# A routed expert layer: experts ranked by their tokens on the chip, with 128, 64 or 32 slots for each

## The reference

```python
h = h + mixed @ w_out
ht = rms_norm(h, g_ffn)                        # 256 tokens x 1024
scores = sigmoid(ht @ w_router)                # 64 experts
biased = scores + router_bias
# the 4 best of 8 groups of experts (sum of the two best of each), then the 8 best experts in them
w = w / sum(w) * 2.5                           # the scores of the 8 chosen
gate = sum(one_hot(idx, 64) * w, axis=1)
a, b = ht @ e_w1[e], ht @ e_w3[e]              # 1024 x 256 each, for each expert e
routed = sum over e of (silu(a) * b * gate[:, e]) @ e_w2[e]     # 256 x 1024
out = h + routed + (silu(ht @ s_w1) * (ht @ s_w3)) @ s_w2       # one shared expert
```

## Time and profile before

| what | value |
|---|---|
| runs | 708.69 us median of 3 (705.74 to 709.54) |
| profiled execution, its own time | 705.52 us |
| its span | 703.8 us |
| mean granted TensorE clock | 0.979 |
| loads of expert weights from batch 0 on | from 118.9 us |
| first expert product | 195.7 us |
| HBM read | 232.85 MB |

### The profile page before, as it was taken

How to read it: one execution, slowest core, us unless ns; L and a number is a source line. 1 busy time by engine, 2 the same in 40 slices (tenths; PEclk the granted TensorE clock), 3 DMA queues, 4 the chain that set the end, 5 groups by cost and what they waited for, 6 DMA issues and landing times.

```text
span 703.8 us, 11436 instructions
## 1 busy us (share of the span) xinstructions
PE 660.4 (94%) x4381; PEld 301.8 (43%) x4381; DVE 328.5 (47%) x762; ACT 203.9 (29%) x376; POOL 22.2 (3%) x40
## 2 busy tenths in 40 slices
PE   3999989999899999999999889998898999989995
PEld 2455466646444434434434333443333434334342
DVE  3999851246814354353443433435334353443435
ACT  5132553202314224133232240422314133141321
POOL 2100031000200000000000000000000000000000
PEclk9999999997999999999999999999999999999999
DMA  9934451961259999999999999999999999999952
GB/s 226 345 117 195 61 190 62 424 248 60 90 209 381 423 408 391 422 420 424 419 423 423 420 423 422 421 422 420 424 422 421 423 420 423 423 420 423 420 209 61
DMA packets 48692, 235.37 MB, mean 334 GB/s; under 512 B 16112, under 2 KB 16144, under 8 KB 21904
## 3 DMA queue, kind: packets, MB, share of 16 engines
q1 hardware_dynamic: 48224, 235.07, 83.8%
q10 hardware_dynamic: 288, 0.02, 0.0%
q0 software_dynamic: 160, 0.00, 0.0%
HBM read 232.85 MB, written 1.05 MB: 332 GB/s over the span
## 4 chain that ended last, share of the span: by engine, by line
PE 56%; DMA 33%; DVE 4%; ACT 2%; issue 2%; SPq 2%; POOL 0%; ACTq 0%; DVEq 0%
PE bank L452 54%; DMA ring<-in_e_w 32%; SPq L319 1%; DMA ring<-in_d_skip 1%; SPq L320 1%; PE bank L776 1%; DVE wreg L1424 1%; DVE reg_d L1107 0%; DVE wreg L1107 0%; ACT reg_c L876 0%; DVE acc L1107 0%; PE bank L514 0%; ACT reg_a L876 0%; POOL reg_d L417 0%; DVE wreg L1110 0%
## 5 line engine op out<-in xcount | busy, mean ns | idle before, releaser
L452 PE MATMUL bank<-ring,wreg 128*64 128x512 f32 (+1 forms) x2128 | 366.0, 600 | 15.9 <-DMA ring<-in_e_w 15.3
L452 PEld LDWEIGHTS bank<-ring,wreg 128*64 128x64 f32 (+1 forms) x2128 | 110.2, 124 | 235.1 <-issue 206.4
L452 PE MATMUL bank<-wreg,reg_a 128*128 128x512 f32 (+1 forms) x224 | 95.2, 587 | 2.9 <-ACT reg_a L876 1.5
L1107 DVE TENSOR_TENSOR wreg<-wreg,bank 128x256 f32<-128x256 f32 x34 | 14.3, 422 | 165.2 <-ACT wreg L1038 165.2
L1113 DVE SCALAR_TENSOR_TENSOR reg_d<-bank,wreg,reg_b 128x512 f32<-128x512 f32 x68 | 47.9, 746 | 60.5 <-ACT reg_b L876 58.5
L1038 ACT ACTIVATE wreg<-bank 128x256 f32<-128x256 f32 x34 | 13.1, 384 | 197.6 <-PE bank L452 197.6
L452 PEld LDWEIGHTS bank<-wreg,reg_a 128*128 128x128 f32 x224 | 43.2, 212 | 47.3 <-issue 45.5
L876 ACT ACTIVATE reg_b<-bank,wreg 128x512 bf16<-128x512 f32 x68 | 43.0, 683 | 62.7 <-PE bank L452 62.7
L1107 DVE TENSOR_TENSOR reg_d<-reg_d,reg_b 128x1024 bf16<-128x1024 f32 x34 | 41.6, 1225 | 38.2 <-ACT reg_b L876 38.2
L452 PE MATMUL bank<-wreg,reg_c 128*128 128x128 bf16 x864 | 55.0, 219 | 1.1 <-DVE wreg L1497 0.8
L452 PEld LDWEIGHTS bank<-wreg,reg_c 128*128 128x128 bf16 x864 | 50.0, 98 | 5.0 <-ACT wreg L876 3.2
(11 more groups left out here) (181 smaller groups left out, 417.6 us busy)
## 6 DMA issues: line engine op xcount, KB each, us to landing
ring<-in_e_w SPq DMA_DIRECT2D x200, 1024.0 KB, 15.7
wreg<-in_w_in SPq DMA_DIRECT2D x4, 2048.0 KB, 14.3
wreg<-in_w_out SPq DMA_DIRECT2D x1, 4096.0 KB, 13.0
wreg<-in_s_w SPq DMA_DIRECT2D x3, 1024.0 KB, 7.2
wreg<-in_e_w SPq DMA_DIRECT2D x3, 1024.0 KB, 4.9
acc<-in_x SPq DMA_DIRECT2D x4, 256.0 KB, 4.8
wreg<-in_w_glu SPq DMA_DIRECT2D x1, 1024.0 KB, 5.3
reg_a<-in_e_w SPq DMA_DIRECT2D x1, 1024.0 KB, 10.4
```

Source lines behind the costliest of these rows:

```text
L452: return nc.tensor.matmul(out_, lhsT, rhs, start=start, stop=stop, **kw)
L1107: return nc.vector.tensor_tensor(out_, a, b, op)
```

## The change

Experts 0 to 7 keep their fixed places (batches 0 and 1). The other 56 are ranked on the chip by their tokens in both halves together. The first 4 are wide: two items of one expert (64 slots for each half, 128 columns) on one load of its weights. The next 28 are plain, one item each, as before. The last 24 are small: one item with 32 slots for both halves together (32 columns). What doesn't fit gets extra items as before. The order is: batches 0 and 1 plain (experts 0 to 7), 2 small, 3 wide (two experts), 4 small, 5 wide (two experts), then the plain ones and the extra items in a loop, and the remaining four batches of small ones.

A small batch has one product `up` with four column tiles of 32, one turn, and one `down` for both halves. The sort (`sort_experts`, `take_list` on VectorE, `count_extras`, `list_items` on TensorE) stands behind the first product of batch 0. The first gather waits for pgT_evac instead of route_ready. SP reads every expert number from batch 2 on into a register (`listed`), and loads batches 2 to 6 by `load_slots`. The shared expert's down product goes into the combine of the first of the last small batches. The tail batch of two items is gone.

```diff
+N_FIXED = 8
+N_WIDE = 4
+N_SMALL = 24
+N_PLAIN = E - N_FIXED - N_WIDE - N_SMALL
+MAX_EXTRA = 88
+N_AHEAD = 2
+FIRST_PLAIN = (N_FIXED + PLAIN_AT) // EB + N_AHEAD
+N_NORMAL = FIRST_PLAIN + N_PLAIN // EB
+N_LAST = N_SMALL // EB - N_AHEAD
+FIRST_BATCHES = ("plain", "plain", "small", "wide", "small", "wide")
...
@@ SP @@
-            load13(ringV[:, 0, 0:4096], 2 * EB, w13_in[0])
+            sp.wait_ge(S["route_ready"], 1)
+            smalls = listed(SMALL_AT)
+            load13(ringV[:, 0, 0:4096], smalls[0], w13_in[0])
             for s in early2:
-                load2(ringV[:, s, 4096:6144], 2 * EB + s, w2_in[s])
-            load_batch(list(range(2 * EB, 3 * EB)), 1, early13, early2)
-            with sp.Fori(3, NB) as b:
-                load_batch([b * EB + s for s in range(EB)], b - 1)
...
+                load2(ringV[:, s, 4096:6144], smalls[s], w2_in[s])
+            load_batch(smalls, 1, early13, early2)
+            def load_slots(before, *loads):
+                sp.wait_ge(S["up_done"], before * NPAIR + NPAIR)
+                for experts_of, pair in loads:
+                    for s in pair:
+                        load13(ringV[:, s, 0:4096], experts_of[s], w13_in[s])
+                sp.wait_ge(S["down_done"], before * 2 + 2)
+                for experts_of, pair in loads:
+                    for s in pair:
+                        load2(ringV[:, s, 4096:6144], experts_of[s], w2_in[s])
+            wides = listed(0, 2)
+            smalls = listed(SMALL_AT + EB)
+            plains = listed(PLAIN_AT)
+            load_slots(2, (wides, (0, 1)), (smalls, (2, 3)))
+            load_slots(3, (smalls, (0, 1)))
+            load_slots(4, (wides, (2, 3)), (plains, (0, 1)))
+            load_slots(5, (plains, (2, 3)))
+            x_before = sp.value_load(n_before[0:1, :], min_val=N_NORMAL - 2, max_val=N_NORMAL - 2 + MAX_FULL)
+            with sp.Fori(FIRST_PLAIN, x_before + 1) as before:
+                load_batch(listed(before * EB + (EB + PLAIN_AT - FIRST_PLAIN * EB)), before)
+            load_batch(listed(SMALL_AT + N_AHEAD * EB), x_before + 1)
+            with sp.Fori(1, N_LAST) as s:
+                load_batch(listed(s * EB + (SMALL_AT + N_AHEAD * EB)), x_before + s + 1)
...
@@ TensorE @@
-            pe.wait_ge(S["cnt_done"], 1)
-            mm(ps[6][0:E, 2 * E + 2:2 * E + 3], tri_b[0:E, 0:E], more_b[0:E, :])
-            mm(ps[6][:, 2 * E + 3:2 * E + 4], ones_b[0:E, :], more_b[0:E, :]).then_inc(S["first_done"], 1)
+            def count_extras():
+                pe.wait_ge(S["cnt_done"], 1)
+                mm(ps[5][0:E, 508:509], tri_b[0:E, 0:E], more_b[0:E, :])
+                mm(ps[5][:, 509:510], ones_b[0:E, :], more_b[0:E, :]).then_inc(S["first_done"], 1)
+            def list_items():
+                pe.wait_ge(S["selx_ready"], 1)
+                pe.wait_ge(S["pgT_evac"], 1)
+                pe.wait_ge(S["rx_ready"], 1)
+                for a in range(2):
+                    mm(ps[4][:, RANKED * a:RANKED * a + RANKED], pgT[:, a, :], selx[0:E, :], True, False)
+                    mm(ps[4][:, RANKED * a:RANKED * a + RANKED], ones_b[0:E, :], offs[0:E, :], False, True)
+                    mm(ps[5][:, RANKED * a:RANKED * a + RANKED], pgT[:, 2 + a, :], selx[0:E, :])
+                mm(ps[4][:, 2 * RANKED:2 * RANKED + N_SMALL], pgT[:, 4, :], selx[0:E, SMALL_AT:RANKED])
+                mm(ps[5][0:1, 2 * RANKED:3 * RANKED], e_col[0:E, :], selx[0:E, :]).then_inc(S["extra_done"], 1)
...
-            pe.wait_ge(S["route_ready"], 1)
+            pe.wait_ge(S["pgT_evac"], 1)
             gather_slices(0)
...
+                if kind == "small":
+                    w13, arrived, count = zip(*(weights13(li[i], slots[i]) for i in range(EB)))
+                    for e in range(EB):
+                        pe.wait_ge(arrived[e], count[e])
+                    for k in range(KT):
+                        for e in range(EB):
+                            last = mm(ps[0][32 * e:32 * e + 32, :], xTg[:, k, 32 * e:32 * e + 32],
+                                      w13[e][:, :, k, :], k == 0, k == KT - 1)
+                    last.then_inc(S["up_done"], 2)
+                    return
...
+            def batch(before, kind="plain", was="plain", then="plain", shared=False):
...
+                up(it, 0, before, kind)
+                if before is None:
+                    count_extras()
+                    list_items()
+                else:
+                    combine(before, was, shared)
+                turn_slots(it, kind)
+                if kind != "small":
+                    up(it, 1, before, kind)
+                turn(it, 0, 2 if kind == "small" else 1)
...
+                for a in range(1 if kind == "small" else 2):
...
+                    down(it, a, before, kind)
...
@@ VectorE @@
+            def sort_experts():
+                c = slice(0, E)
+                dve.wait_ge(S["rx_ready"], 1)
+                step(nc.vector.tensor_copy(cnt2[c, :], ps[4][c, 0:2]))
+                tt(most[c, :], cnt2[c, 0:1], cnt2[c, 1:2], ALU.max)
+                step(tt(cnt[c, :], cnt2[c, 0:1], cnt2[c, 1:2], ALU.add))
+                row = ps[4][c, E:2 * E]
+                ts(beats, row, cnt[c, :], ALU.is_gt)
+                ts(over32[c, :], cnt[c, :], float(SLOTS), ALU.is_gt)
+                step(stt(ties, row, cnt[c, :], tri_b[c, 0:E], ALU.is_equal, ALU.mult))
+                step(tt(beats, beats, ties, ALU.add))
+                step(nc.vector.tensor_reduce(rank[c, :], beats[:, N_FIXED:E], AX.X, ALU.add))
...
+                nc.vector.tensor_copy(more_b[c, :], more[c, :]).then_inc(S["cnt_done"], 1)
...
+            def batch(before, kind="plain", then="plain", at=None):
                 it = 0 if before is None else before + 1
+                by = 2 if kind == "small" else 1
+                activate(it, 0, by)
+                if before is None:
+                    sort_experts()
+                    take_list()
...
```

More of the change, by code:

```diff
@@ L734, in gather_slices @@
+            def gather_slices(n, small=False):
                 for k in (2 * n, 2 * n + 1):
@@ L769, in up, with turn @@
                 last.then_inc(S["up_done"], 1)
-            def turn(it, p):
+            def turn(it, p, by=1):
                 pe.wait_ge(S["act_ready"], it * NPAIR + (p + 1))
@@ L807, in combine @@
                     for hf in range(2):
+                        bank = ps[y_bank(a) + hf]
+                        if shared:
+                            pe.wait_ge(S["sh_actT"], 2)
+                            for j in range(2):
+                                mm(bank[:, :], actT_s[a][:, j, :], sh2[:, j, 512 * hf:512 * hf + 512], j == 0, False)
                         for w in range(3):
-                            last = mm(ps[y_bank(a) + hf][:, :], PT[:, a, :], y_parts[w][:, a, 512 * hf:512 * hf + 512],
-                                      w == 0, w == 2)
+                            last = mm(bank[:, :], PT[:, a, :], y_parts[w][:, 0 if kind == "small" else a, 512 * hf:512 * hf + 512],
+                                      w == 0 and not shared, w == 2)
@@ L842, in batch @@
-                gather_slices(3)
-                for a in range(2):
-                    if before is not None:
+                if then is not None:
+                    pe.wait_ge(S["P_ready"], it + 2)
+                    gather_slices(0, small)
+                    gather_slices(1, small)
+                if kind != "small":
+                    turn(it, 1)
+                if then is not None:
+                    pe.wait_ge(S["xa"], it * 2 + 3)
+                    gather_slices(2, small)
+                    pe.wait_ge(S["xd"], it * 2 + 3)
+                    gather_slices(3, small)
@@ L852, in _ @@
-            n_it = pe.value_load(n_iter[0:1, :], min_val=NB, max_val=MAX_FULL)
-            tail = pe.value_load(n_tail[0:1, :], min_val=0, max_val=1)
-            with pe.Fori(1, last_full) as before:
-                batch(before)
-            pe.wait_ge(S["xa"], n_it * 2 + 2)
-            pe.wait_ge(S["xd"], n_it * 2 + 2)
-            shared_down()
-            combine(last_full)
-            with pe.If(tail > 0):
-                pe.wait_ge(S["acc_added"], n_it * 4)
-                turn_slots(n_it)
-                up(n_it, 0)
-                turn(n_it, 0)
-                pe.wait_ge(S["gm_dve"], n_it + 1)
-                pe.wait_ge(S["acc_added"], n_it * 4 + 4)
-                down(n_it, 0, 2)
-                down(n_it, 1, 2)
-                combine(n_it)
+            for it in range(1, FIRST_PLAIN):
+                batch(it - 1, FIRST_BATCHES[it], FIRST_BATCHES[it - 1],
+                      FIRST_BATCHES[it + 1] if it + 1 < FIRST_PLAIN else "plain")
@@ new lines, in _ @@
+            x_before = pe.value_load(n_before[0:1, :], min_val=N_NORMAL - 2, max_val=N_NORMAL - 2 + MAX_FULL)
+            with pe.Fori(FIRST_PLAIN - 1, x_before) as before:
+                batch(before)
+            batch(x_before, then="small")
```

(14 more changed lines are left out.)

439 lines of the change are left out of this document (222 added, 217 removed).

## The result

The changed kernel takes **711.88 us** (median of 12 runs, 710.78 to 715.56) against 706.07 us for the kernel before on the same chip (12 runs, 703.69 to 709.54): ratio 1.0078, 95% interval 1.0058 to 1.0097. It is slower by 5.8 us; 700.8 was forecast, faster. That forecast was 7.9 us under a median of three runs; under the median of twelve it would be 698.2. The profiled execution took 712.7 us, with a span of 710.8. Against the span of before, 703.8, that is 7.0 more.

The account below looks back on a forecast made before the run. TensorE bounds the first five batches, the DMA the rest. Gains of 29.8 us less load, 2.4 of tail and under 1 of landing, against about 25 more idle DMA, gave -7.9 us: 700.8 from 708.7, range 690 to 712.

Parts of the forecast that it names:

- about 25 more idle DMA: Whole span: new idle DMA at the front and around small batches, about 25 us, set against 29.8 us less load.
- The tail's gain: End of kernel: shared down product moved away and half a y-chain; last down to end 14.4 for 16.8, gain 2.4 us.
- The bound: Whole kernel: TensorE sets the pace for the first five batches at 27.8 us, the DMA afterwards at 29.83.
- rival E: Batch count: extra items remain, so a whole plain batch more, 27.8 us, about 724; chance 0.02.
- The sort: In front of batch 0's second product: 11.3 us where 0.6 stood, 13.0 with one clock fall, bounds 9 and 15.
- rival D: Small batch's up product: four column tiles of four experts don't run abreast, at worst 14.2 us, about 738; chance 0.03.
- SP's list reads: SP before batch 3's loads: twelve register reads, at most 1.3 us each, 11 us free; nothing taken, bound +4.
- The front: Batches 0 and 1: first product at 192.8, then the sort; 15 us of nothing between two pieces of batch 1's weights.
- Idle DMA at the two early small batches: Batches 2 and 4: the DMA idles 6 us at each, clock cost included.
- The clock after a wait: Small products after long waits: slowed by TensorE's lowered clock, 1.7 us each, bounds 0 and 7.1.
- Rival C: Small batches' first products stay long at 1.2 GHz: break-even 3.0 us per product, full 7.1 about 728; chance 0.10.
- Rival B: TensorE's early work gives all back: sort 15, clock 2.5 per product, 703.0 on the span, -1; chance 0.20.

Follow-up runs that it names:

- E4: Changed kernel with dummy products, whose result nobody reads, filling TensorE's waits before the six small products: 704.44 us, ratio 0.998 to the kernel before.
- E1: Changed kernel with the sort and list products moved behind batch 0's second product: 701.85 us, ratio 0.994 to the kernel before.
- E13: E1 plus small products in two pairs, no dummies, and early release of first spaces in wide and early small batches: 689.97 us, ratio 0.9782.
- E3: Changed kernel with each small product in two pairs of experts, space freed per pair in the last four batches only: 708.55 us, ratio 1.0036.
- E10: E7 plus the small product in two pairs of experts as in E3: 711.23 us, ratio 1.0053 to the kernel before.
- E12: E7 with each wide batch giving up its first expert's space after its first product: 694.39 us, ratio 0.9819 to the kernel before.
- E7: Changed kernel with the edits of E1 and E4 together: 695.38 us, ratio 0.9823 to the kernel before.

## Why the prediction was wrong

Sign and size were wrong; 711.88 lies just inside the stated range of 690 to 712, on the wrong side of no change. On the profiled span I had 695.9 and 710.8 came, 14.9 more: 6.0 by batch 6 (367.1 for 361.1), 3.3 from there to batch 12, 5.5 from there to batch 16, nothing behind it.

**The step that failed** is the sum's term "about 25 more idle DMA": it is 37, which is 12 of the 14.9. By stretch, more idle DMA than in the kernel before, forecast and measured: 12 and 8.8 us up to 222 us, 12 and 16.5 up to 340, 0 and 3.0 up to 480, 3 and 8.4 up to 677 (the forecast's parts add up to 27, the measured ones to 37). The 29.8 us less of loads were right. The tail's gain, 0.6 us instead of 2.4, is most of the rest.

- **Held.** The bound. 192 loads and 17 batches: rival E is out. The sort: 12.0 us for 11.3 (its listed parts add up to 10.9), and 2.3 for the slow clock behind it (9.35 for 7.09). The four tiles of four experts abreast, 7.07 us at full clock in E4: rival D is out. SP's list reads made it issue batch 2's load at 233.72, 3.2 us after 229.75 + 0.80, and that lay in free time.
- **The front: right, and dear.** Between the two pieces of batch 1's weights the DMA stood still for 16.2 us (204.0 to 220.8 us, 14 GB/s), 15 were forecast, and batch 1 began at 229.6 for 230.5. The first product came at 190.64, 2.2 us before the forecast; 1.8 of that is luck, since the whole mixer ran earlier in this execution (the first expert load at 117.10 for 118.92). I had priced the sort and not asked whether it could stand elsewhere: E1 prices its place at 10.0 us (11.7 without small batches), so that without it the change would have shown 5 us faster, with all other errors in it.
- **When weights are there.** I let a load be there when all bytes issued up to it have moved at 422 GB/s. For batch 2 that gives 262.3 (16 MB issued from 219.1 us on: 220.8 + 1.7 idle + 39.8), which is my start of batch 2 (262.4); they landed at 264.9. The next two loads, w2, issued from 257.36 on, and the DMA around them:
```profile
DMA to landing us min/median/max: 10.0/11.1/12.1
...
265.00:267.00 2.00, 1.94 (x12) 0.50 0.96 397
268.00:269.00 1.00, 1.00 (x8) 0.52 0.12 49
```
  They landed at 267.4 and 269.9, so the order of issue held. But from 220.8 to 265.0 the DMA had moved 403 GB/s, which is 17.0 of the 18 MB issued by then (1 MB is 1.049 million bytes), where batch 2 needs 16: most DMA engines were moving w2 already while the slowest had batch 2's last load to finish, and from 268 to 269 us only two of the sixteen (share 0.12) were at work. Each load landed in sixteen parts; of batch 2's last one fourteen were there by 263.3 and two at 264.9. So the product starts later, and there is less of w2 left to move beside it. Batch 16 has the same: 8 MB issued from 653.04 on give 653.0 + 1.7 + 19.9 = 674.6, and they landed at 676.7 (656.92 + 19.74); by the same sum batches 14 and 15 lost 0.6 us each. The Trainium skill, DMA: Bandwidth & Descriptors, section "Queues, rings and completion order", states that completion is not first in, first out even for one issuing engine. Load by load it was here, and the page gives no time for it.
- **Idle DMA at the two early small batches**: 6 + 6 us forecast, 8.5 (260 to 290 us) and 8.7 (320 to 350) measured. w2 was to cover a small batch's product; at batch 2 all but 1 MB of it had already come with the rest, and ahead of batch 4 it is two experts' only. E13 has 4.8 us less of it than E1 from 222 to 340 us (374 GB/s for 357).
- **The clock after a wait**: 1.7 us per product was taken, with 0 and 7.1 as bounds. Measured over 7.07, with the wait for weights before it:

| batch | 2 | 4 | 13 | 14 | 15 | 16 |
|---|---|---|---|---|---|---|
| wait, us | 7.8 | 4.8 | 13.3 | 4.4 | 11.4 | 12.8 |
| product over 7.07, us | 1.9 | 2.7 | 1.3 | 2.9 | 2.0 | 2.5 |

  That is 2.2 on average; 0.5 more than I took is 3 us in all by my own sensitivity. The mechanism was right and the term too small, and it does not grow with the wait: the two shortest waits cost most. E4 prices all of it at 7.4 us. The last two periods were 32.5 and 33.0 for 30.8, over the 32 that I had named as a sign of being wrong. Rival C's place was the right one, but at 2.2 us a product and not the 3.0 at which it decides alone.
- **From batch 6 on** TensorE set the pace for three periods of 27.8 us (358.53 to 441.94 in the chain) and not for five. Why the DMA's pace ruled two batches sooner was not traced and stays open.
- **The tail**: last down to end 710.8 - 694.6 = 16.2 for 14.4, since the last combination runs at half clock too (700 to 702 us). That batch 16 to the end still took 34.0 us for 33.9 is luck: my time line had 31.5 there, and the 2.4 us by which it had ended too early on the old kernel filled the gap.

The page that spoke against me (the Trainium skill, TensorE: Matmul & The Clock Gate, section "Measured speedup vs the span model", 2.38x for three column tiles) led, by my estimate from it, to 9.0 us a product and about 707. Products of 9.0 us did come, and for another reason: the clock stood at 0.50 in their first 2 us, and E4 has 7.07. A figure can fit for the wrong reason; the same product in two states of the clock tells.

Rival B was nearest in its terms (sort 15, clock 2.5 each): sort and clock together came to 14.3, and it gave 703.0 on the span. It lacks the late landings and the small batches' idle time.

## What to carry to other kernels

Loads saved are worth something only where the queue has something else to load: count the idle DMA that each new order of the work opens (space given back all at once, a step that holds up the only engine that frees space) against the megabytes saved, and before anything else ask for what batch a new result is first needed; here the list wasn't before batch 2, and moving it was 10 us. Where an engine has to wait for weights anyway, split its work so that part of it lies in the wait, and see to it that the space of the first part is given free at once; where it doesn't wait, the split of 4 column tiles into 2 and 2 costs 5.2 us (12.25 for 7.07). An improvement that fills a wait is spent only once: dummies and halves together took 16 us more than dummies alone, in part because two of the six split products gave no space free. And weights are there when the slowest DMA engine has its part, not when the mean rate says so.

## What the runs showed of the hardware

- 32 records of two 32-column tiles abreast took 7.06 us and 64 records of four abreast 7.07 (E3, E4); two pairs, one behind the other without a wait, 12.25 for 64 records (E10).
- After waits for weights of 4.4 to 13.3 us TensorE ran the first 2 us of the six small products at a granted clock of 0.50 (1.2 GHz), and they took 1.3 to 2.9 us longer, the most after the shortest wait. Behind dummies and waits of 0.8 to 3.2 us the product took 7.07 us in three of the last four small batches of E4 and in all four of E12, but 8.4 to 8.8 us in three of the four of E7, behind waits of 2.9 to 3.3.
- The 1 MB loads of this trace landed in sixteen parts, one or two of them often behind the others: batch 2's last load had fourteen by 263.3 us and the last at 264.9. Loads landed in their order of issue, 264.9, 267.4 and 269.9, though by 265.0 the DMA had moved 17.0 of their 18 MB.
- Four reads of the list by SP took at most 3.2 us together, 0.8 each.
